# Other begins within a 64 byte line for the operands of three feed-forward stages

## The chip, the cores and the metric

The kernel runs on one core of a Trainium2 chip. The time is that of one execution on the device in microseconds (us), as a median of three runs. The core's engines are TensorE (PE in the profile; its loading of weights has a row of its own, PEld), VectorE (DVE), ScalarE (ACT), GpSimd (POOL) and SyncE (SP), which issues most of the DMAs. All operands lie in the on-chip memory SBUF: 128 partitions, in each of which a tensor occupies a run of bytes. Where such a run begins is what this change is about.

## The reference

A float32 network for 512 positions of width 1024. First four layers, each a mixer (hyena, window attention, pooling, hyena) and a gated feed-forward with an inner width of 2816; then a second block (a gated delta rule beside latent attention, their merge, and a feed-forward with an inner width of 4096). What the change touches are feed-forwards 1 and 2 of the first block and the last feed-forward:

```
def swiglu(xn, wg, wu, wd):
    return (jax.nn.silu(xn @ wg) * (xn @ wu)) @ wd

x = x + swiglu(rmsnorm(x, norm_ffn[i]), ff_w_gate[i], ff_w_up[i], ff_w_down[i])   # layers 0 to 3
...
x = x + mod_x[5] * _sq_relu_mlp(_modulate(_rms(x, norm_mlp[l]), mod_x[3], mod_x[4]), w_mlp_in[l], w_mlp_out[l])
```

## The kernel before, in words

Activations are kept transposed: a row is a tile of 128 features by 512 positions, one feature to a partition, 2048 bytes in each. A matmul takes a weight tile of 128 by 128 (512 bytes in each partition) as its stationary operand and one row as the moved one, 512 columns, and adds into a PSUM bank.

The large products are split. Each operand is written as a high part, rounded to the format fp32r, and a low part, which is what the rounding left, and three fp32r matmuls replace a float32 one (lines 963 to 965): high weights by high rows, high weights by low rows, low weights by high rows. Each of them has its own weight load. So one step over k reads, in this order, `x_hi` with `w_hi`, `x_lo` with `w_hi`, `x_hi` with `w_lo`. The other float32 products of the kernel (lines 1463, 1477 and others) are not split; each of them stands in the trace as two matmuls, the two passes of a float32 product.

A feed-forward (`split_layers`, line 989) runs in parts: two for `ffn`, four for `mlp`. A part has an "in" phase, blocks of weights for two output tiles each, 48 matmuls to a block (11 blocks in `ffn`, 4 in `mlp`), which makes the hidden rows, and an "out" phase of 8 blocks, one output tile each (33 matmuls to a block in `ffn`, 24 in `mlp`), which reads the hidden rows `h_hi` and `h_lo`. A feed-forward has 1584 of these matmuls, the last stage 1536.

Blocks of weights come by DMA from the array `stream` into `ring`, which has four places. ScalarE copies a block rounded into `w_hi` (line 1900), GpSimd writes `w_lo` = ring minus `w_hi` (line 817), and TensorE waits for that. `w_hi` and `w_lo` have two halves, taken in turn by `j % 2`: ScalarE may write half `j % 2` when the matmuls of block j-2 have ended. VectorE writes `x_lo` (lines 2515 and 2520), `h_hi` and `h_lo` (2525 and 2526). All the queues run in the order in which the program was written; each engine's order is fixed by hand.

Tensors lie in SBUF one behind the other in the order of their declaration. `lines` (line 304) rounds the small ones up to 64 elements, 256 bytes, and `before_x` fills 128 bytes so that `x` begins at byte 1280. In the built program every operand of the split products begins at a multiple of 256 bytes. `w_hi`, `x_lo`, `h_hi`, `h_lo`, `w_lo` and `x_hi` lie behind one another in a work area that the other stages use for other things at other times. Feed-forwards 0 and 3 follow a hyena mixer, whose last weights still lie in this area.

Of the kernel before, what the change touches and what calls it, by code (L numbers as in the profile page):

```python
# [24 lines left out]
LINE = 64  # L25
HEAD_GAP = 32
# [265 lines left out]
def build_program(nc, stream, vecs, tabs, tabs2, x_in, ctx_in, first_mods, scratch, x_keep, diag, solved_t, solved_n, out, schedule):  # L292
# [4 lines left out]
    with ExitStack() as stack:  # L297
# [11 lines left out]
        sb("before_x", [P, HEAD_GAP])  # L309
# [444 lines left out]
        def _(pool):  # L754
# [50 lines left out]
            def split(stage, blocks_):  # L805

                def run_(arg):
                    first = starts[(stage, arg)]
                    for j in range(blocks_):
# [7 lines left out]
                        nc.gpsimd.tensor_tensor(w_lo[:, j % 2, 0:cols], ring[:, k % RING, 0:cols], w_hi[:, j % 2, 0:cols],  # L817
# [81 lines left out]
        def _(pe):  # L899
# [82 lines left out]
            def split_weights(j):  # L982

                blk.take()
                n["split"] += 1
                pe.wait_ge(wlo_set, n["split"])
                return [w[:, j % 2, :].rearrange("p (w m) -> p w m", m=P) for w in (w_hi, w_lo)]

            def split_layers(parts, blocks_in, kt_out, mods=False, between=None):

                j = 0
                first = n["xn"] - DT
                for _ in range(parts):
                    for f in range(blocks_in):
                        hi, lo = split_weights(j)
# [8 lines left out]
                    for m in range(DT):  # L1004
                        hi, lo = split_weights(j)
                        split_product(hi, lo, 0, h_hi, h_lo, kt_out, (hidden_set, n["hid"]) if m == 0 else None)
                        j += 1
                    n["hid"] += kt_out

            def ffn(layer):  # L1010
                split_layers(2, FT // 2, FT // 2, True, {2: column_sums, 5: rstd_spread})
# [834 lines left out]
            def mlp(_):  # L1846
                split_layers(4, 4, DT)
# [14 lines left out]
        def _(act):  # L1862
# [30 lines left out]
            def split(stage, arg, j):  # L1893
# [6 lines left out]
                signal(go(w_hi[:, j % 2, 0:cols], ring[:, k % RING, 0:cols], ACT.Copy), whi_set)  # L1900
# [17 lines left out]
            def scaled(k, t, gain):  # L1918
                act.wait_ge(acc_drained[acc.place(t)], acc.turn(t) + 1)
                signal(go(x_hi[:, k, :], x[:, k, :], ACT.Identity, scale=V(gain[0], gain[1] + k)), xhi_set)  # L1920

            def norm(gain, then=None):
# [554 lines left out]
        def _(dve):  # L2477
# [28 lines left out]
            def low(k, high=x_hi, out_=x_lo):  # L2506
# [1066 lines left out]
```

## Time and profile before

| | us |
|---|---|
| median of three runs (lowest, highest) | 4314.81 (4314.14, 4316.48) |
| the profiled execution | 4315.63 |
| its span, first to last instruction | 4313.8 |
| feed-forwards 0 to 3, first to last matmul | 363.8, 363.8, 365.3, 363.8 |
| the last stage, first to last matmul | 356.6 |
| mean granted TensorE clock | 0.957 of full speed |

In a matmul's row the duration is the time from its start to its modelled end. Neighbouring matmuls overlap, so the rate of TensorE is read from the distance of their starts, here called the pitch, and not from the durations. A `x24` in a row of the timeline means that 24 instructions of one form stand in a sequence.

### The profile page before, as it was taken

To read this page: it belongs to the slowest core of one execution; us is meant where nothing else is said; L and a number is where in the kernel's file an instruction comes from. 1 tells how busy PE (TensorE), PEld (TensorE's weight loads), DVE (VectorE), ACT (ScalarE), POOL (GpSimd) and SP (SyncE) were. 2 spreads that over 40 slices of the span, in tenths; PEclk is the share of its full clock that TensorE was granted. 3 is DMA by queue.
4 is the path that set the end of the run, shared out by engine and by line. 5 is a ranking of instruction groups with operands and counts; after the bars stand their busy time and mean duration, and the time that the engine had idled before them with its cause. 6 is when DMAs were issued, how large, how long until landed. Compare 5 with 4: busy or idle time off the path is not lost.

```text
span 4313.8 us, 48957 instructions
## 1 busy us (share of the span) xinstructions
PE 4104.3 (95%) x19446; PEld 3122.4 (72%) x19446; DVE 2207.2 (51%) x3161; ACT 1271.7 (29%) x1756; POOL 1493.9 (35%) x845
## 2 busy tenths in 40 slices
PE   7998999999999999999989998999999999999999
PEld 6655888777888888876568886566666666785887
DVE  6588525475515442576875144566663357404322
ACT  3332222355222322233322222323231234422222
POOL 3311444321444244433124441465663000231443
PEclk9998999999999899999989998999998889999999
DMA  6201332311232223222013321112111111222232
GB/s 185 100 30 40 111 111 83 116 40 69 83 118 85 85 85 124 89 73 88 30 50 126 120 78 68 50 34 58 35 36 55 70 69 69 69 97 72 89 105 76
DMA packets 101075, 341.94 MB, mean 79 GB/s; under 512 B 44400, under 2 KB 47600, under 8 KB 72176
## 3 DMA queue, kind: packets, MB, share of 16 engines
q1 hardware_dynamic: 87968, 311.60, 20.9%
q10 hardware_dynamic: 12880, 27.20, 2.3%
q8 instruction: 155, 2.54, 0.2%
q14 instruction: 72, 0.59, 0.0%
HBM read 321.48 MB, written 17.30 MB: 79 GB/s over the span
## 4 chain that ended last, share of the span: by engine, by line
PE 84%; DVE 10%; ACT 2%; POOL 2%; issue 1%; DMA 0%; SPq 0%; DVEq 0%; ACTq 0%; POOLq 0%
PE bank L963 17%; PE bank L965 17%; PE bank L964 17%; PE bank L1463 5%; PE bank L1175 2%; PE bank L1087 1%; PE bank L1443 1%; PE bank L1165 1%; PE bank L1083 1%; PE bank L927 1%; PE bank L1764 1%; PE bank L1763 1%; PE bank L1785 1%; PE bank L1695 1%; PE bank L1724 1%
## 5 line engine op out<-in xcount | busy, mean ns | idle before, releaser
L817 POOL TENSOR_TENSOR w_lo<-ring,w_hi 128x2048 fp32r<-128x2048 f32 (+2 forms) x200 | 775.6, 3878 | 1187.4 <-ACT w_hi L1900 1158.3
L963 PE MATMUL bank<-x_hi,w_hi 128*128 128x512 f32 x1584 | 617.8, 390 | 3.9 <-POOL w_lo L817 3.9
L965 PE MATMUL bank<-x_hi,w_lo 128*128 128x512 f32 x1584 | 616.7, 389 | 0.0
L964 PE MATMUL bank<-x_lo,w_hi 128*128 128x512 f32 x1584 | 616.6, 389 | 0.0
L1900 ACT ACTIVATE w_hi<-ring 128x2048 fp32r<-128x2048 f32 (+2 forms) x200 | 322.2, 1611 | 713.3 <-PE bank L965 712.3
L963 PE MATMUL bank<-h_hi,w_hi 128*128 128x512 f32 x960 | 374.1, 390 | 0.4
L964 PE MATMUL bank<-h_lo,w_hi 128*128 128x512 f32 x960 | 373.7, 389 | 0.0
L965 PE MATMUL bank<-h_hi,w_lo 128*128 128x512 f32 x960 | 373.7, 389 | 0.0
L963 PEld LDWEIGHTS bank<-x_hi,w_hi 128*128 128x128 f32 x1584 | 297.5, 188 | 66.5 <-POOL w_lo L817 5.2
L964 PEld LDWEIGHTS bank<-x_lo,w_hi 128*128 128x128 f32 x1584 | 297.5, 188 | 61.6
L965 PEld LDWEIGHTS bank<-x_hi,w_lo 128*128 128x128 f32 x1584 | 297.4, 188 | 61.6
L830 POOL TENSOR_TENSOR ring_r<-ring,merge_hi 128x2048 fp32r<-128x2048 f32 x16 | 73.5, 4591 | 494.7 <-ACT merge_hi L2415 494.7
L1463 PE MATMUL bank<-xn,ring 128*128 128x512 f32 x496 | 239.2, 621 | 1.4 <-DVE work L2946 1.4
L2587 DVE TENSOR_TENSOR x<-bank,x 128x512 f32<-128x512 f32 x72 | 49.8, 691 | 355.9 <-PE bank L965 344.5
L963 PEld LDWEIGHTS bank<-h_hi,w_hi 128*128 128x128 f32 x960 | 180.2, 188 | 39.3 <-DVE h_lo L2526 2.0
L964 PEld LDWEIGHTS bank<-h_lo,w_hi 128*128 128x128 f32 x960 | 180.3, 188 | 37.4
L965 PEld LDWEIGHTS bank<-h_hi,w_lo 128*128 128x128 f32 x960 | 180.2, 188 | 37.3
L1978 ACT ACTIVATE xn<-xn 128x512 f32<-128x512 f32 x88 | 55.7, 632 | 453.9 <-DVE xn L2600 453.8
L2600 DVE TENSOR_TENSOR xn<-bank,rstd_t 128x512 f32<-128x512 f32 x88 | 60.8, 691 | 194.1 <-PE bank L965 187.4
L799 POOL TENSOR_TENSOR tab<-tab 56x31 f32<-56x31 f32 (+15 forms) x248 | 151.0, 609 | 19.4
L1463 PEld LDWEIGHTS bank<-xn,ring 128*128 128x128 f32 x496 | 92.7, 200 | 89.8 <-issue 88.6
L854 POOL TENSOR_TENSOR work<-work,ring 128x1024 f32<-128x1024 f32 x32 | 76.7, 2427 | 226.1 <-DVE x L2653 171.1
(527 smaller groups left out, 7889.2 us busy)
## 6 DMA issues: line engine op xcount, KB each, us to landing
ring<-stream SPq DMA_DIRECT2D x211, 1024.0 KB, 4.8
ring<-stream SPq DMA_DIRECT2D x64, 704.0 KB, 4.0
ring<-stream SPq DMA_DIRECT2D x36, 512.0 KB, 3.4
xn<-first_mods SPq DMA_DIRECT2D x8, 1024.0 KB, 6.8
x<-x_keep ACTq DMA_DIRECT2D x3, 2048.0 KB, 8.6
ring<-stream SPq DMA_DIRECT2D x4, 1088.0 KB, 4.9
bias_rows<-work ACTq DMA_DIRECT2D x1, 4096.0 KB, 45.9
x_keep<-x ACTq DMA_DIRECT2D x2, 2048.0 KB, 11.0
```

The source lines that it names most:

```text
L799: solve(tt(part, G[:, 0:i, i:i + 1].broadcast_to([56, i, w]), W[:, i:i + 1, i:SUB].broadcast_to([56, i, w]), ALU.mult))
L817: nc.gpsimd.tensor_tensor(w_lo[:, j % 2, 0:cols], ring[:, k % RING, 0:cols], w_hi[:, j % 2, 0:cols], ALU.subtract).then_inc(wlo_set, 1)
L830: nc.gpsimd.tensor_tensor(ring_r[:, w, 0:2 * DT * P], ring[:, w, 0:2 * DT * P], merge_whi[j % 2][:], ALU.subtract).then_inc(wlo_set, 1)
L854: nc.gpsimd.tensor_tensor(pair, pair, factor[:, r:r + 1, :].broadcast_to([P, 2, 512]), ALU.mult).then_inc(filt_set, 1)
L963: mm(b[:], hi[:, at + k, :], rhs_hi, start=(k == 0), stop=False)
L964: mm(b[:], hi[:, at + k, :], rhs_lo[:, k, :], start=False, stop=False)
L965: ins = mm(b[:], lo[:, at + k, :], rhs_hi, start=False, stop=(k == kt - 1))
L1175: ins = mm(b[:], fwd[term], filt[:, kind, term[1], :], start=(j == 0), stop=(j == 1))
L1463: ins = mm(b[:, 0:TC] if ctx else b[:], w[:, at + k, :], src[:, k, :], start=(k == 0), stop=(k == DT - 1))
L1900: signal(go(w_hi[:, j % 2, 0:cols], ring[:, k % RING, 0:cols], ACT.Copy), whi_set)
L1978: signal(go(gate_tmp[:, f % 2, :], gate_tmp[:, f % 2, :], ACT.Silu), silu_set)
L2600: drain(tt_(gate, bank(t)[:], rstd, ALU.mult), t)
```

## The change

Nothing is added, removed or moved: each engine has the same instructions in the same order, with the same waits. What differs is where tensors begin.

- `LINE` goes from 64 to 16 elements and `before_x` goes away, so the small tensors take less room and everything behind them moves down by 128 to 960 bytes. Each tensor still begins at a multiple of 64 bytes, most of them no longer at one of 256.
- `w_hi` and `w_lo` become two tensors each, one for a half. For feed-forwards 0 and 3 (`EVEN`) the eight pieces lie behind one another as before.
- For feed-forwards 1 and 2 and the last stage the pieces lie in a second layout (names that end in `_at`) over the same area, with 64 bytes of room behind each, and the operands begin some elements into their piece, by the table `BEGIN`. The high rows, `x_hi` and `h_hi`, stay at 0.

The table, written out in elements of 4 bytes past a multiple of 64 bytes:

| stage, phase | low rows | half 0: w_hi, w_lo | half 1: w_hi, w_lo |
|---|---|---|---|
| ffn 1, in | 4 | 0, 0 | 4, 4 |
| ffn 1, out | 8 | 0, 0 | 0, 8 |
| ffn 2, in | 0 | 4, 4 | 8, 8 |
| ffn 2, out | 0 | 2, 2 | 12, 4 |
| last, in | 12 | 0, 0 | 8, 4 |
| last, out | 6 | 0, 0 | 4, 2 |

A row is 2048 bytes and a weight tile 512, so every row and every tile of a tensor begins at the same place of its line.

```diff
-LINE = 64
-HEAD_GAP = 32
+LINE = 16
+PARTS = dict(ffn=FT // 2, mlp=DT)
+PHASE_BLOCKS = dict(ffn=(FT // 2, DT), mlp=(4, DT))
+EVEN = ((0, ((0, 0), (0, 0))), (0, ((0, 0), (0, 0))))
+BEGIN = {
+    ("ffn", 0): EVEN,
+    ("ffn", 1): ((4, ((0, 0), (4, 4))), (8, ((0, 0), (0, 8)))),
+    ("ffn", 2): ((0, ((4, 4), (8, 8))), (0, ((2, 2), (12, 4)))),
+    ("ffn", 3): EVEN,
+    ("mlp", 0): ((12, ((0, 0), (8, 4))), (6, ((0, 0), (4, 2)))),
+}
...
-        sb("before_x", [P, HEAD_GAP])
...
-        w_hi, x_lo, h_hi, h_lo, w_lo, x_hi = [
-            stack.enter_context(nc.sbuf_tensor(name, shape, F32R)) for name, shape in (
-                ("w_hi", [P, 2, 2 * DT * P]), ("x_lo", [P, DT, T]), ("h_hi", [P, FT // 2, T]), ("h_lo", [P, FT // 2, T]),
-                ("w_lo", [P, 2, 2 * DT * P]), ("x_hi", [P, DT, T]))]
+        pieces = (("w_hi0", 2 * DT * P), ("w_hi1", 2 * DT * P), ("x_lo", DT * T), ("h_hi", FT // 2 * T), ("h_lo", FT // 2 * T),
+                  ("w_lo0", 2 * DT * P), ("w_lo1", 2 * DT * P), ("x_hi", DT * T))
+
+        def split_pieces(ending, room):
+            with ExitStack() as over:
+                return {name: over.enter_context(nc.sbuf_tensor(name + ending, [P, size + room], F32R)) for name, size in pieces}
+
+        even_area = split_pieces("", 0)
+        odd_area = split_pieces("_at", LINE)
+        work_end = stack.enter_context(nc.sbuf_tensor("work_end", [P, WORK + len(pieces) * LINE], F32))
+
+        def area(stage, arg):
+            return even_area if BEGIN[stage, arg] is EVEN else odd_area
+
+        def split_rows(name, stage, arg, tiles):
+            at = BEGIN[stage, arg][name[0] == "h"][0] if name.endswith("lo") else 0
+            return area(stage, arg)[name][:, at:at + tiles * T].rearrange("p (a b) -> p a b", a=tiles)
+
+        def split_halves(stage, arg, j):
+            ins, outs = PHASE_BLOCKS[stage]
+            at = BEGIN[stage, arg][j % (ins + outs) >= ins][1][j % 2]
+            return [area(stage, arg)[f"{name}{j % 2}"][:, at[i]:at[i] + 2 * DT * P] for i, name in enumerate(("w_hi", "w_lo"))]
...
-                        nc.gpsimd.tensor_tensor(w_lo[:, j % 2, 0:cols], ring[:, k % RING, 0:cols], w_hi[:, j % 2, 0:cols],
+                        high, low = split_halves(stage, arg, j)
+                        nc.gpsimd.tensor_tensor(low[:, 0:cols], ring[:, k % RING, 0:cols], high[:, 0:cols],
                                                 ALU.subtract).then_inc(wlo_set, 1)
...
-                signal(go(w_hi[:, j % 2, 0:cols], ring[:, k % RING, 0:cols], ACT.Copy), whi_set)
+                signal(go(split_halves(stage, arg, j)[0][:, 0:cols], ring[:, k % RING, 0:cols], ACT.Copy), whi_set)
```

The rest of the diff hands `stage` and `arg` to the functions that read or write these tensors.

## Rows read from the trace of the kernel before

**Rows 1.** The page: span, and engine, busy us (share of the span), instructions.

```profile
span 4313.8 us, 48957 instructions
...
PE 4104.3 (95%) x19446; PEld 3122.4 (72%) x19446; DVE 2207.2 (51%) x3161; ACT 1271.7 (29%) x1756; POOL 1493.9 (35%) x845
```

**Rows 2.** The page's chain that ended last, shares of the span by engine.

```profile
PE 84%; DVE 10%; ACT 2%; POOL 2%; issue 1%; DMA 0%; SPq 0%; DVEq 0%; ACTq 0%; POOLq 0%
```

**Rows 3.** The page's costliest groups: busy, mean ns | idle before, releaser.

```profile
L817 POOL TENSOR_TENSOR w_lo<-ring,w_hi 128x2048 fp32r<-128x2048 f32 (+2 forms) x200 | 775.6, 3878 | 1187.4 <-ACT w_hi L1900 1158.3
L963 PE MATMUL bank<-x_hi,w_hi 128*128 128x512 f32 x1584 | 617.8, 390 | 3.9 <-POOL w_lo L817 3.9
L965 PE MATMUL bank<-x_hi,w_lo 128*128 128x512 f32 x1584 | 616.7, 389 | 0.0
L964 PE MATMUL bank<-x_lo,w_hi 128*128 128x512 f32 x1584 | 616.6, 389 | 0.0
...
L963 PE MATMUL bank<-h_hi,w_hi 128*128 128x512 f32 x960 | 374.1, 390 | 0.4
```

**Rows 4.** Busy time by stretch: feed-forwards 0 to 3, then the last stage.

```profile
core 0: us, PE busy (x) PEld busy (x) DVE busy (x) ACT busy (x) POOL busy (x), PEclk, DMA share, GB/s
443.90:807.70 363.80, 363.80 (x1625) 301.69 (x1623) 151.58 (x172) 85.25 (x72) 155.18 (x38) 1.00 0.30 104
1061.40:1425.20 363.80, 363.80 (x1625) 301.75 (x1623) 148.92 (x173) 83.33 (x71) 151.94 (x37) 1.00 0.30 104
1475.10:1840.40 365.30, 365.30 (x1625) 302.81 (x1625) 148.60 (x172) 83.95 (x71) 155.83 (x38) 1.00 0.30 104
2262.90:2626.70 363.80, 363.80 (x1625) 301.70 (x1623) 147.24 (x172) 83.33 (x71) 152.03 (x37) 1.00 0.29 101
3948.90:4305.50 356.60, 352.27 (x1536) 289.05 (x1536) 119.10 (x141) 84.32 (x84) 140.83 (x46) 0.99 0.24 80
```

**Rows 5.** Line 964, second half of feed-forward 0: durations, first and last start.

```profile
L964 PEld LDWEIGHTS bank<-h_lo,w_hi x88: 187/188/188, 747.8 to 806.9; 128*128 128x128 f32 x88
L964 PE MATMUL bank<-h_lo,w_hi x88: 388/389/390, 748.0 to 807.2; 128*128 128x512 f32 x88
```

**Rows 6.** TensorE in order of time, last stage: start us, us, instruction.

```profile
4100.10 0.39 PE L963 MATMUL bank<-h_hi,w_hi 128*128 128x512 f32 x1
4100.32 0.39 PE L964 MATMUL bank<-h_lo,w_hi 128*128 128x512 f32 x1
4100.55 0.39 PE L965 MATMUL bank<-h_hi,w_lo 128*128 128x512 f32 x1
4100.78 0.39 PE L963 MATMUL bank<-h_hi,w_hi 128*128 128x512 f32 x1
...
4104.18 0.39 PE L963 MATMUL bank<-h_hi,w_hi 128*128 128x512 f32 x1
```

**Rows 7.** Weight loads of the same stretch.

```profile
4100.10 0.19 PEld L964 LDWEIGHTS bank<-h_lo,w_hi 128*128 128x128 f32 x1
4100.33 0.19 PEld L965 LDWEIGHTS bank<-h_hi,w_lo 128*128 128x128 f32 x1
4100.55 0.19 PEld L963 LDWEIGHTS bank<-h_hi,w_hi 128*128 128x128 f32 x1
4100.78 0.19 PEld L964 LDWEIGHTS bank<-h_lo,w_hi 128*128 128x128 f32 x1
```

**Rows 8.** TensorE in order of time, two-pass float32 products, 512 and 256 columns.

```profile
2730.48 10.47 PE L1463 MATMUL bank<-xn,ring 128*128 128x512 f32 x24
2740.78 3.62 PE L1463 MATMUL bank<-work,ring 128*128 128x256 f32 x16
2744.24 2.31 PE L1463 MATMUL bank<-xn,ring 128*128 128x512 f32 x5
```

**Rows 9.** TensorE in order of time, attention: fp32r products of 256 columns.

```profile
897.12 0.28 PE L1217 MATMUL bank<-at_whi,x_hi_a 128*128 128x256 f32 x1
897.23 0.28 PE L1218 MATMUL bank<-ring_r,x_hi_a 128*128 128x256 f32 x1
...
899.27 0.28 PE L1217 MATMUL bank<-at_whi,x_hi_a 128*128 128x256 f32 x1
```

**Rows 10.** TensorE in order of time, recurrent stage: moved tiles at two begins.

```profile
2716.69 0.61 PE L1477 MATMUL bank<-tab,work 128*128 128x128 f32 x4
2717.14 0.39 PE L1473 MATMUL bank<-work 128*128 128x128 f32 x2
2717.36 0.61 PE L1477 MATMUL bank<-tab,work 128*128 128x128 f32 x4
```

**Rows 11.** ScalarE groups by shape.

```profile
L1900 ACT ACTIVATE w_hi<-ring 128x2048 fp32r<-128x2048 f32 x104 | 199.8, 1921 | 283.4 <-PE bank L965 282.7
```

**Rows 12.** GpSimd groups by shape.

```profile
L817 POOL TENSOR_TENSOR w_lo<-ring,w_hi 128x2048 fp32r<-128x2048 f32 x104 | 488.9, 4701 | 746.2 <-ACT w_hi L1900 717.1 <-DVE x_lo L2515 29.1
L817 POOL TENSOR_TENSOR w_lo<-ring,w_hi 128x1408 fp32r<-128x1408 f32 x64 | 210.3, 3285 | 313.1 <-ACT w_hi L1900 313.1
...
L817 POOL TENSOR_TENSOR w_lo<-ring,w_hi 128x1024 fp32r<-128x1024 f32 x32 | 76.5, 2389 | 128.1 <-ACT w_hi L1900 128.1
```

**Rows 13.** Who TensorE waited for in the last stage: us, times, longest.

```profile
PE bank L963 <- POOL w_lo L817: 3.9, 3, 1.3
PE bank L974 <- DVE x_lo L2520: 2.7, 1, 2.7
```

**Rows 14.** Line 817: duration min/median/max, first and last start.

```profile
L817 POOL TENSOR_TENSOR w_lo<-ring,w_hi x200: 2387/4575/5153, 433.0 to 4295.9; 128x2048 fp32r<-128x2048 f32 x52, 128x1408 fp32r<-128x1408 f32 x32, 128x1024 fp32r<-128x1024 f32 x16
```

More of the change, by code:

```diff
@@ L980, in split_pair, with split_weights @@
                         between[k]()
-            def split_weights(j):
+            def split_weights(stage, arg, j):
                 blk.take()
@@ L986, in split_weights, with split_layers @@
                 pe.wait_ge(wlo_set, n["split"])
-                return [w[:, j % 2, :].rearrange("p (w m) -> p w m", m=P) for w in (w_hi, w_lo)]
-            def split_layers(parts, blocks_in, kt_out, mods=False, between=None):
+                return [w.rearrange("p (w m) -> p w m", m=P) for w in split_halves(stage, arg, j)]
+            def split_layers(stage, arg, parts, blocks_in, kt_out, mods=False, between=None):
                 j = 0
+                x_hi, x_lo = [split_rows(name, stage, arg, DT) for name in ("x_hi", "x_lo")]
+                h_hi, h_lo = [split_rows(name, stage, arg, kt_out) for name in ("h_hi", "h_lo")]
                 first = n["xn"] - DT
@@ L994, in split_layers @@
                     for f in range(blocks_in):
-                        hi, lo = split_weights(j)
+                        hi, lo = split_weights(stage, arg, j)
                         if j == 0:
@@ L1010, in ffn @@
             def ffn(layer):
-                split_layers(2, FT // 2, FT // 2, True, {2: column_sums, 5: rstd_spread})
+                split_layers("ffn", layer, 2, FT // 2, FT // 2, True, {2: column_sums, 5: rstd_spread})
             def hyena(s):
@@ L1919, in scaled @@
                 act.wait_ge(acc_drained[acc.place(t)], acc.turn(t) + 1)
-                signal(go(x_hi[:, k, :], x[:, k, :], ACT.Identity, scale=V(gain[0], gain[1] + k)), xhi_set)
+                signal(go(split_rows("x_hi", "ffn", gain[1] // DT, DT)[:, k, :], x[:, k, :], ACT.Identity, scale=V(gain[0], gain[1] + k)), xhi_set)
             def norm(gain, then=None):
@@ L2504, in full, with low @@
                 return t
-            def low(k, high=x_hi, out_=x_lo):
+            def low(k, high, out_):
                 n["xhi"] += 1
@@ L2514, in scaled_low @@
                 dve.wait_ge(xhi_set, n["xhi"])
-                signal(stt(x_lo[:, k, :], x[:, k, :], V(gain[0], gain[1] + k), x_hi[:, k, :], ALU.mult, ALU.subtract), xn_set)
+                high, out_ = [split_rows(name, "ffn", gain[1] // DT, DT) for name in ("x_hi", "x_lo")]
+                signal(stt(out_[:, k, :], x[:, k, :], V(gain[0], gain[1] + k), high[:, k, :], ALU.mult, ALU.subtract), xn_set)
             def shifted_low(k, shift):
@@ L2519, in shifted_low, with split_hidden @@
                 dve.wait_ge(xhi_set, n["xhi"])
-                signal(stt(x_lo[:, k, :], xn[:, k, :], modv[:, shift + k, 0:1], x_hi[:, k, :], ALU.add, ALU.subtract), xn_set)
-            def split_hidden(f):
+                high, out_ = [split_rows(name, "mlp", 0, DT) for name in ("x_hi", "x_lo")]
+                signal(stt(out_[:, k, :], xn[:, k, :], modv[:, shift + k, 0:1], high[:, k, :], ALU.add, ALU.subtract), xn_set)
+            def split_hidden(stage, arg, f):
                 h = h_tmp[:, f % 2, :]
+                h_hi, h_lo = [split_rows(name, stage, arg, PARTS[stage]) for name in ("h_hi", "h_lo")]
                 step(nc.vector.tensor_copy(h_hi[:, f, :], h))
@@ L2605, in ffn @@
                         drain(tt_(h_tmp[:, f % 2, :], bank(t)[:], gate_tmp[:, f % 2, :], ALU.mult), t)
-                        split_hidden(f)
+                        split_hidden("ffn", layer, f)
                         if f in MOD_SUMS:
```

8 lines of the change are left out of this document (4 added, 4 removed).

## The prediction

> **What bounds the kernel now.** I read the page first: TensorE is busy for 95% of the span [rows 1], and the chain that ended last is 84% TensorE [rows 2]. The reader is to see that no other engine can pay for a change here. The costliest groups are the three products of a split step, 1584 + 960 of each, and the idle time ahead of them is 3.9 us and less [rows 3]. By stretches, feed-forwards 0 to 3 take 363.8, 363.8, 365.3 and 363.8 us and the last stage 356.6, all at a granted clock of 0.99 or 1.00, that is at 2.4 GHz, with TensorE busy throughout [rows 4]. The three changed stages are thus 363.8 + 365.3 + 356.6 = 1085.7 us, a quarter of the time, and they hold 1584 + 1584 + 1536 = 4704 split matmuls.
>
> A duration of 390 ns says nothing of the rate, since neighbours overlap. The pitch does: in the last stage 18 pitches lie between 4100.10 and 4104.18 us, 226.7 ns each [rows 6]; in feed-forward 0, 261 pitches lie between the first and last of 88 starts, 59.2 us or 226.8 ns [rows 5]. At 2.4 GHz 512 columns are 213.3 ns. So each split matmul costs 13.3 ns on top of its columns. The fp32r products of 256 columns have 18 pitches in 2.15 us, 119.4 ns, where 256 columns are 106.7: again some 13 ns, so it is an amount per matmul, not a rate [rows 9]. The passes of the unsplit float32 products have pitches of 10.30 us / 24 = 429.2 and 3.46 / 16 = 216.3 ns: their columns go at half the rate (426.7 and 213.3) with about 2.7 ns on top [rows 8]. The weight load of the next matmul starts together with the running one and is over in 190 ns, inside the pitch of 227 [rows 6, 7]. What the change can touch is this overhang: 13.3 - 2.7 = 10.6 ns that only rows streamed at the full rate pay, from columns that are read while weights are read too, all begun at a multiple of 64 bytes.
>
> **The change part by part.** *Instructions:* none is added or moved, so no wait or queue changes; 0 us.
>
> *Low rows begun off the line.* `x_lo` and `h_lo` are displaced for feed-forward 1 (352 in, 176 out) and the last stage (256 and 256): 1040 of the 4704 matmuls move such a row. A row of 2048 bytes touches 33 lines of 64 bytes instead of 32. If the reading goes by such lines, one takes 213.3 / 32 = 6.7 ns at the full rate, and there is nothing to hide it, because the pitch is set by the row: 1040 x 6.7 = +6.9 us. If the line isn't the unit, 0. The trace has no fp32r row off the line. It has float32 tiles of 128 columns off it: line 1473 moves a tile that begins 48 bytes into its line under weights that do so too, line 1477 moves one at 0 under weights at 0, and four of the one take 0.45 us, two of the other 0.22, 112 and 110 ns each [rows 10]. That speaks for 0, but those tiles go at half the rate. I take +1 us, near the row, and keep 0 and 6.9.
>
> *Weights begun off the line.* A load of 512 bytes touches 9 lines instead of 8. It ends 190 ns into a pitch of 227 [rows 7], so up to 37 ns more are hidden: 0. Without that cover each displaced load would cost what it is over.
>
> *Rows and weights at different places of a line.* This is what the table varies. In the order of the reads, a moved row has the load of the next weights beside it: `x_hi` with `w_hi`, `x_lo` with `w_lo`, `x_hi` with `w_hi`. Counting where the two begin at different places: 176 + 352 (ffn 1, in), 88 + 0 (ffn 1, out), 1584 (ffn 2), 128 + 384 and 128 + 384 (last stage), together 3224. If the overhang is a clash of two reads at the same place, they lose up to 10.6 ns each: -34 us. If being at one place is what keeps it small, they gain as much or more: doubled, +34 us. Bounds -34 and +34. The nearest rows, again [rows 10], show no dependence, and the pitch is the same, 226.7, in stages whose rows and weights lie in quite different tensors [rows 5, 6]. I take 0.
>
> The Trainium skill, "SBUF — State Buffer", Who interferes with whom, says that TensorE has two independent read ports, one for the moving operand and one for weights; by that there is no clash and this term is 0. "TensorE: Matmul & The Clock Gate", Back-to-back issue gap, gives N / 2.4 + 2.5 ns, 215.8 for 512 columns; the float32 passes above fit it with their doubled columns, the split matmuls don't, by 10.9 ns. So the pages do not explain the very overhang that this change plays with, and I do not rest on the first rule alone.
>
> *The writers.* ScalarE, GpSimd and VectorE write displaced tensors. A block is rounded in 1.92 us [rows 11] and subtracted in 4.70 [rows 12], 6.6 us, against 48 x 0.2267 = 10.9 us of matmuls for an in block and 33 x 0.2267 = 7.5 for an out block of a feed-forward. Only at the last stage's step from out to in the cover is short, 24 x 0.2267 = 5.4 us, and there TensorE waits today, 3.9 us in 3 times [rows 13]. Were displaced copies slower by the spread of line 817, 5.15 against 4.70 [rows 12, 14], that would be 3 x 0.45 = +1.4 us. I take 0. Faster matmuls would lengthen these waits by 3 x 24 x 0.0106 = 0.8 us.
>
> *All tensors moved down, to multiples of 64 instead of 256 bytes.* The trace has no operand of a split product that isn't at a multiple of 256. If the unit were longer than 64 bytes, feed-forwards 0 and 3 and the mixers would pay as well, with a 33rd of a row, 6.7 ns on each of some 10,000 matmuls, +67 us. Nothing in rows favours that; I take 0 and keep the bound as a rival.
>
> **Sum.** Against the profiled execution: span 4313.8 + 1.8 around it = 4315.6 us; + 1 = 4316.6. The median of the runs is 0.8 lower, 4314.8, so the forecast is 4316 us.
>
> **The rivals.** *Rival 1, the clash is real and is resolved.* For it: the overhang of 10.6 ns exists only where the row is streamed at the full rate, is the same for 256 and 512 columns, as the weight load is, and the rest of the kernel hides it at half rate. Against it: the load runs within each pitch whatever lies where, and its length isn't changed by the begin. With half of the bound, -17 us: 4298; with all of it, 4281. It decides from 8.6 / 3224 = 2.7 ns per matmul.
>
> *Rival 2, slower: rows that begin off the line, or off the place of the weights, break the stream.* A row at the full rate has no slack in which to fetch a second piece; each matmul that it hits gets a longer pitch at once, on the chain. For it: the full-rate stream already pays what the half-rate one doesn't. Against it: [rows 10]. With the overhang doubled on the 1040 displaced low rows, 1040 x 13.3 = +14 us: 4329. On the 3224 with differing places, +34 to +43: 4349 to 4358. At worst the displaced rows fall to the half rate, 1040 x 203 = +211 us. It decides from 8.3 ns on the 1040 or 2.7 ns on the 3224.
>
> *Rival 3, the unit is longer than a line of 64 bytes.* +67 us as worked out, 4382; its mark is that feed-forwards 0 and 3 get longer too.
>
> *By a rule of short lines:* a slower pitch could come only from begins inside a 16 byte line, the 256 out rows of the last stage at element 6, one line of 1.7 ns each, 0.4 us. "SBUF — State Buffer", Specifications, gives SBUF such 16-byte lines. This lies inside the forecast.
>
> **How the numbers follow.** A measurement of this kernel tells apart about 0.2%, 8.6 us. Forecast (0 to +6.9 us, 4313 to 4323): 0.46. Rival 1: 0.26. Rival 2: 0.25. Rival 3: 0.03. Of rival 1 some 0.02 stays within 0.2%, of rival 2 some 0.01. Different begins in twelve places may also pull both ways and cancel, which I count with the forecast. Faster 0.24, same 0.49, slower 0.27. The range leaves out the last fifth of rival 1 (below 4285) and the upper part of rivals 2 and 3 (above 4348): 4285 to 4348. The likeliest case alone: 4313 to 4323.
>
> **What would show it.** Right: feed-forwards 1 and 2 and the last stage again 364, 365 and 357 us, and a pitch of 226.7 ns in all twelve places of the table, with perhaps 233 where a displaced low row is moved. Wrong by rival 1: pitches of 216 to 224 where row and weights differ, and 226.7 where they begin alike (ffn 1, out, half 1), which stays as a control inside the run. Wrong by rival 2: pitches over 230 in the third of the matmuls on line 964 alone, or on all three lines. Feed-forwards 0 and 3 stay at 363.8 in each case but the third. A VectorE, ScalarE or GpSimd group that grew, with TensorE waiting for it, would overturn the term of the writers.

## The result, and the profile after

The changed kernel takes 4350.19 us (median of three, 4347.10 to 4359.28) against 4314.81: a ratio of 1.0086, interval 1.0062 to 1.011. It is slower by 35 us, and the prediction, 4316 with a range of 4285 to 4348, was wrong; the median lies 2 us above the range. The profiled execution took 4347.10 us, its span is 31.5 us longer than that of before.

The page after, in the order of [rows 1] and [rows 3]: span; engines; costliest groups with busy us, mean ns, idle before.

```profile
span 4345.3 us, 48957 instructions
...
PE 4130.2 (95%) x19446; PEld 3111.1 (72%) x19446; DVE 2201.5 (51%) x3161; ACT 1271.4 (29%) x1756; POOL 1496.2 (34%) x845
...
L845 POOL TENSOR_TENSOR w_lo_at<-ring,w_hi_at 128x2048 fp32r<-128x2048 f32 (+2 forms) x124 | 459.7, 3708 | 776.6 <-ACT w_hi_at L1930 768.6
L845 POOL TENSOR_TENSOR w_lo<-ring,w_hi 128x2048 fp32r<-128x2048 f32 (+1 forms) x76 | 317.0, 4171 | 432.0 <-ACT w_hi L1930 412.4
L991 PE MATMUL bank<-x_hi_at,w_hi_at 128*128 128x512 f32 x912 | 361.6, 396 | 3.5 <-POOL w_lo_at L845 3.5
L992 PE MATMUL bank<-x_lo_at,w_hi_at 128*128 128x512 f32 x912 | 359.8, 394 | 0.0
L993 PE MATMUL bank<-x_hi_at,w_lo_at 128*128 128x512 f32 x912 | 358.2, 393 | 0.0
L991 PE MATMUL bank<-x_hi,w_hi 128*128 128x512 f32 x672 | 261.8, 390 | 0.0
```

The instructions are the same in number, TensorE has 26 us more of busy time and no other engine has grown by more than GpSimd's 2.3 us: GpSimd's two groups make 776.7 us together, against 775.6 in [rows 3], and TensorE waits for them 3.5 us instead of 3.9. The matmuls themselves take longer: in the moved stages 393 to 396 ns each, in the two that were left alone 390 as before.

Feed-forwards 0 to 3 and the last stage after, to be held against [rows 4]:

```profile
core 0: us, PE busy (x) PEld busy (x) DVE busy (x) ACT busy (x) POOL busy (x), PEclk, DMA share, GB/s
445.50:809.30 363.80, 363.75 (x1625) 301.63 (x1623) 152.43 (x172) 85.16 (x72) 157.47 (x38) 1.00 0.29 104
1063.50:1436.40 372.90, 372.90 (x1625) 302.17 (x1623) 148.56 (x172) 83.27 (x71) 152.32 (x37) 1.00 0.29 101
1480.20:1856.50 376.30, 376.28 (x1624) 303.19 (x1624) 148.57 (x174) 83.96 (x71) 151.72 (x38) 0.99 0.28 100
2280.80:2644.60 363.80, 363.77 (x1625) 301.63 (x1623) 148.05 (x172) 83.25 (x71) 154.17 (x37) 1.00 0.29 101
3972.60:4336.80 364.20, 360.65 (x1536) 289.44 (x1536) 118.55 (x141) 84.31 (x84) 141.35 (x46) 0.99 0.23 78
```

The granted clock is that of before, 0.99 to 1.00. Feed-forwards 0 and 3 have not changed. The three moved stages are longer, and from the start of the first matmul to that of the last (the ends are modelled) the traces give +9.0, +11.0 and +7.5 us, together 27.5. (Feed-forward 2 takes 365.7 to 366.1 us in e1 and e7 to e9 below, where nothing in it is displaced, against 364.9 before, so about 1 us of its 11.0 is no matter of the layout.) That is 27.5 / 4704 = 5.8 ns per split matmul.

Matmuls in order of time (start us, us), and one row of line 991 by count, first and last start. First feed-forward 0, then the last six pitches of feed-forward 1, then the last stage; against [rows 5] and [rows 6]:

```profile
L991 PE MATMUL bank<-h_hi,w_hi x88: 389/389/389, 749.2 to 808.4; 128*128 128x512 f32 x88
...
1434.61 0.40 PE L993 MATMUL bank<-h_hi_at,w_lo_at 128*128 128x512 f32 x1
1434.84 0.40 PE L991 MATMUL bank<-h_hi_at,w_hi_at 128*128 128x512 f32 x1
1435.08 0.40 PE L992 MATMUL bank<-h_lo_at,w_hi_at 128*128 128x512 f32 x1
1435.31 0.40 PE L993 MATMUL bank<-h_hi_at,w_lo_at 128*128 128x512 f32 x1
...
1436.02 0.39 PE L993 MATMUL bank<-h_hi_at,w_lo_at 128*128 128x512 f32 x1
...
4100.11 0.40 PE L991 MATMUL bank<-x_hi_at,w_hi_at 128*128 128x512 f32 x1
...
4102.21 0.40 PE L991 MATMUL bank<-x_hi_at,w_hi_at 128*128 128x512 f32 x1
```

Feed-forward 0: 59.2 us / 261 = 226.8 ns, as before. At the end of feed-forward 1, in the blocks that the prediction named as its control, 1.41 us / 6 = 235 ns. In the last stage 2.10 / 9 = 233 ns. In most steps all three products are longer, also that of `x_hi` with `w_hi` where both tensors begin at element 0 of their piece. Not everywhere: in the half 0 blocks of feed-forward 1's out phase the third product, `h_hi` with `w_lo`, keeps 226.8 ns (mean of 88), while the step as a whole takes 693 ns instead of 680.

The rest of the 31.5 us lies outside the feed-forwards. From the same two traces, in us:

| stretch | before | after | difference |
|---|---|---|---|
| start to feed-forward 0 | 443.9 | 445.5 | +1.6 |
| feed-forwards 0 and 3 | 727.0 | 726.7 | -0.3 |
| mixer ahead of ffn 1 | 254.0 | 254.7 | +0.7 |
| feed-forward 1 | 363.5 | 372.5 | +9.0 |
| pooling ahead of ffn 2 | 50.3 | 44.2 | -6.1 |
| feed-forward 2 | 364.9 | 375.9 | +11.0 |
| mixer ahead of ffn 3 | 422.8 | 424.7 | +1.9 |
| second block to its last stage | 1322.6 | 1328.4 | +5.8 |
| last stage | 356.2 | 363.8 | +7.5 |
| behind the last matmul | 8.6 | 8.9 | +0.3 |

The -6.1 is the clock, not the change. The end of the pooling stage, before and then after:

```profile
1457.00:1475.10 18.10, 18.10 (x90) 18.10 (x89) 13.36 (x14) 10.23 (x12) 4.55 (x1) 0.51 0.00 1
```

```profile
1468.00:1480.10 12.10, 9.68 (x87) 9.59 (x86) 11.68 (x13) 9.98 (x12) 4.63 (x1) 0.92 0.10 28
```

Some 90 matmuls in each. Before they ran at a granted 0.51 (the lower level, 1.2 GHz), after mostly at 2.4. In other runs this stretch fell to either side whatever the layout, 44.2 to 53.5 us in all, so I count it as neither gain nor loss. Without it the mixers and the second block cost about +10 us. By these lengths alone that is not certain: among runs in which the split products outside the feed-forwards keep the pitch of before, the second block takes 1321.3 us (e9) to 1327.2 us (e10). The mixers and the second block also hold split products, 2784 of them, whose operands lie in `xn`, `ring` and the work area. A mixer of before and the same of after (lines 974 to 976 have become 1002 to 1004):

```profile
31.00 0.39 PE L974 MATMUL bank<-x_hi_h,early_hi 128*128 128x512 f32 x1
...
32.81 0.39 PE L976 MATMUL bank<-x_hi_h,ring_r 128*128 128x512 f32 x1
```

```profile
31.03 0.40 PE L1002 MATMUL bank<-x_hi_h,early_hi 128*128 128x512 f32 x1
...
32.88 0.39 PE L1004 MATMUL bank<-x_hi_h,ring_r 128*128 128x512 f32 x1
```

Eight pitches each: 226 ns and 231 ns. 2784 x 4.4 = 12 us is what this would cost throughout. Taken pitch by pitch over the two traces (2630 pairs of neighbouring starts, less than 0.3 us apart), the split products outside the feed-forwards take 231.4 instead of 227.3 ns, which is 10.9 us. That is the loss outside the feed-forwards.

**The layout as it was built.** The pitch did not follow the table of begins, so I worked out every operand's byte address modulo 256. Before: 0 for all. After:

| | place modulo 256 bytes |
|---|---|
| `x`, `xn`, `ring` | 128 |
| work area, and the pieces of ffn 0 and 3 | 64 |
| `w_hi0`, `w_hi1`, `x_lo`, `h_hi` of the moved stages | 64, 128, 192, 0 (+ table) |
| `h_lo`, `w_lo0`, `w_lo1`, `x_hi` of the moved stages | 64, 128, 192, 0 (+ table) |

The room of 64 bytes behind each piece moves the next one by a whole line, so rows and weights lie at different places of 256 bytes even where the table says 0 and 0. And the smaller header moved `xn` and `ring` by another amount than the work area. Both stand in the diff; the prediction read past both.

The unsplit float32 products of after, as [rows 8]:

```profile
2748.83 10.46 PE L1493 MATMUL bank<-xn,ring 128*128 128x512 f32 x24
2759.13 3.62 PE L1493 MATMUL bank<-work,ring 128*128 128x256 f32 x16
2762.58 5.74 PE L1493 MATMUL bank<-xn,ring 128*128 128x512 f32 x13
```

10.30 / 24 = 429 and 3.45 / 16 = 216 ns, as before. The first is no test, since `xn` and `ring` both lie at 128; the second is one, for `work` (64) and `ring` (128) now lie at different places. Lines 1195 (`ring` 128, `work` 64) and 1205 (`work` 64, `tab` 192) are one for 512 columns: their starts are 429 ns apart, as before. What slows the split products leaves the half-rate ones alone.

Nor does it slow the fp32r products of 256 columns in the attention stage, to be held against [rows 9]. `x_hi_a` now lies at 64, `ring_r` and `xn_r` at 128 and `at_whi` at 64, so two of the three products have their row and weights at different places:

```profile
899.32 0.28 PE L1247 MATMUL bank<-at_whi,x_hi_a 128*128 128x256 f32 x1
...
901.45 0.28 PE L1247 MATMUL bank<-at_whi,x_hi_a 128*128 128x256 f32 x1
```

18 pitches in 2.13 us are 118.3 ns, against 119.4 before. So the loss is shown for fp32r products of 512 columns only.

### The profile page after: what moved, and what is told of

The parts are those of the page before. It is cut to its first block, busy times and chain, and to the rows that moved or that the text cites. A ratio compares the mean times of both kernels' runs of the same rounds, so it can differ in the third digit from the quotient of the medians.

```text
span 4345.3 us, 48957 instructions
## 1 busy us (share of the span) xinstructions
PE 4130.2 (95%) x19446; PEld 3111.1 (72%) x19446; DVE 2201.5 (51%) x3161; ACT 1271.4 (29%) x1756; POOL 1496.2 (34%) x845
## 4 chain that ended last, share of the span: by engine, by line
PE 84%; DVE 10%; ACT 2%; POOL 2%; issue 1%; DMA 0%; SPq 0%; DVEq 0%; ACTq 0%; POOLq 0%
PE bank L991 18%; PE bank L992 17%; PE bank L993 17%; PE bank L1493 5%; PE bank L1205 2%; PE bank L1117 1%; PE bank L1473 1%; PE bank L1195 1%; PE bank L1113 1%; PE bank L955 1%; PE bank L1794 1%; PE bank L1793 1%; PE bank L1815 1%; PE bank L1725 1%; PE bank L1754 1%
## 5 line engine op out<-in xcount | busy, mean ns | idle before, releaser
L845 POOL TENSOR_TENSOR w_lo_at<-ring,w_hi_at 128x2048 fp32r<-128x2048 f32 (+2 forms) x124 | 459.7, 3708 | 776.6 <-ACT w_hi_at L1930 768.6
L845 POOL TENSOR_TENSOR w_lo<-ring,w_hi 128x2048 fp32r<-128x2048 f32 (+1 forms) x76 | 317.0, 4171 | 432.0 <-ACT w_hi L1930 412.4
L991 PE MATMUL bank<-x_hi_at,w_hi_at 128*128 128x512 f32 x912 | 361.6, 396 | 3.5 <-POOL w_lo_at L845 3.5
L992 PE MATMUL bank<-x_lo_at,w_hi_at 128*128 128x512 f32 x912 | 359.8, 394 | 0.0
L993 PE MATMUL bank<-x_hi_at,w_lo_at 128*128 128x512 f32 x912 | 358.2, 393 | 0.0
L991 PE MATMUL bank<-x_hi,w_hi 128*128 128x512 f32 x672 | 261.8, 390 | 0.0
L992 PE MATMUL bank<-x_lo,w_hi 128*128 128x512 f32 x672 | 261.4, 389 | 0.0
L993 PE MATMUL bank<-x_hi,w_lo 128*128 128x512 f32 x672 | 261.4, 389 | 0.0
L991 PE MATMUL bank<-h_hi_at,w_hi_at 128*128 128x512 f32 x608 | 241.9, 398 | 0.0
L992 PE MATMUL bank<-h_lo_at,w_hi_at 128*128 128x512 f32 x608 | 239.9, 395 | 0.0
```

The lines of the kernel that those rows point to most:

```text
L845: nc.gpsimd.tensor_tensor(low[:, 0:cols], ring[:, k % RING, 0:cols], high[:, 0:cols], ALU.subtract).then_inc(wlo_set, 1)
L991: mm(b[:], hi[:, at + k, :], rhs_hi, start=(k == 0), stop=False)
L992: mm(b[:], hi[:, at + k, :], rhs_lo[:, k, :], start=False, stop=False)
L993: ins = mm(b[:], lo[:, at + k, :], rhs_hi, start=False, stop=(k == kt - 1))
```

## The experiments

Below, "place" is an address modulo 256 bytes, and a stage's length is from its first to its last matmul's start. "Sum of three" is the time from one high by high product to the next, three matmuls: 680 ns in every stage of before, as the median.

**e1: the changed kernel with every stage even.** No room, no table; the small header stays.

```diff
-BEGIN = {
-    ("ffn", 0): EVEN,
-    ("ffn", 1): ((4, ((0, 0), (4, 4))), (8, ((0, 0), (0, 8)))),
...
+BEGIN = {key: EVEN for key in (("ffn", 0), ("ffn", 1), ("ffn", 2), ("ffn", 3), ("mlp", 0))}
```

> The changed kernel with its smaller small tensors (LINE 16, no 128 byte gap), but every stage in the even layout: no room behind the pieces, no begin inside a line. All tensors begin at multiples of 64 bytes; those of the work area are at 320 modulo 512, x, xn and ring at 128. Theory A (pitch is 226.7 ns only where all rows and weights of a step begin at the same place of something longer than 64 bytes): feed-forwards 1, 2 and the last stage go back to 363.5, 365 and 356 us, the mixers and the merge stay at 231.1 ns on 2784 matmuls, 12 us over before: about 4325 us. Theory B (only begins inside a 64 byte line cost): 4315, with 226.7 everywhere; that the mixers' triples of 693 ns in the changed kernel were something else would then have to be shown.

Measured 4325.45 against 4317.02 us, ratio 1.0024 (1.0014 to 1.0033). Feed-forward 1 and the last stage:

```profile
1065.80:1429.60 363.80, 363.74 (x1625) 301.63 (x1623) 149.34 (x172) 83.24 (x71) 154.11 (x37) 1.00 0.30 104
3957.70:4314.80 357.10, 352.47 (x1536) 289.07 (x1536) 119.87 (x141) 84.30 (x84) 142.94 (x46) 0.99 0.24 80
```

The feed-forwards are back, and about a quarter of the loss stays. It lies in the other stages, where the sum of three is 693 ns; counted pitch by pitch as above, their split products take 11.0 us longer than before.

**e2: the changed kernel with 320 bytes of filler ahead of the work area**, so that it lies at the place of `xn` and `ring` (and at the same one modulo 512).

```diff
+        sb("filler", [P, 80])
         with nc.sbuf_tensor("at_whi", [P, 2, 2 * DT * P], F32R) as at_whi:
```

> The changed kernel with 320 bytes of filler ahead of the work area, so that the work area, x, xn and ring all lie at 128 modulo 512; table and rooms of the three changed stages as in the changed kernel. Theory A: mixers and merge return to 226.7 ns, the three stages keep their +9, +11 and +7.5 us: about 4350 - 12 = 4338 to 4342 us. Theory B: no change against the changed kernel, 4350.

Measured 4339.28, ratio 1.0054 (1.0039 to 1.0069). The mixers' sum of three is 680 again, with not one instruction changed in them, only moved by 320 bytes, and their split products take as long as before (0.0 us, counted pitch by pitch). The span is 8.0 us shorter than after's, 4337.3. The three stages keep their loss: 371.8, 375.9, 363.5 us.

**e3: e2 with all begins 0, and only the rooms left.**

```diff
+ZERO = ((0, ((0, 0), (0, 0))), (0, ((0, 0), (0, 0))), "at")
-    ("ffn", 1): ((4, ((0, 0), (4, 4))), (8, ((0, 0), (0, 8)))),
+    ("ffn", 1): ZERO,
...
```

> As the run with the filler, but every begin of the table is 0: no operand begins inside a line. What is left of the change in the three stages is the 64 bytes of room behind each piece, which puts the eight pieces at eight different multiples of 64 modulo 512. Theory A: the stages stay at 231 to 233 ns, within some us of the run with the filler: 4335 to 4342 us. Theory B: 226.7 ns in all stages, 4315 us.

Measured 4344.53, ratio 1.0067 (1.0052 to 1.0082). Feed-forwards 1 and 2, last stage:

```profile
1061.50:1434.90 373.40, 373.40 (x1625) 302.02 (x1623) 148.90 (x173) 83.35 (x71) 152.18 (x37) 1.00 0.29 101
1480.00:1855.80 375.80, 375.76 (x1624) 303.75 (x1624) 149.83 (x174) 83.97 (x71) 156.27 (x38) 0.99 0.29 100
3969.50:4333.90 364.40, 360.81 (x1536) 289.34 (x1536) 118.23 (x141) 84.37 (x84) 141.24 (x46) 0.99 0.24 78
```

The median is 2.5 us above what theory A expected. Every operand begins at a multiple of 64 bytes, no row touches a 33rd line, and the loss of the three stages is whole: 27.8 us against 27.5. So whole lines of distance are enough.

**e5: the table alone.** Pieces put in another order and padded so that all lie at one place modulo 256; what differs are the 8 to 48 bytes of the table.

```diff
+            ("ffn", 1): split_pieces("_at1", ("w_hi0", "x_lo", "w_hi1", "h_lo", "h_hi", "w_lo0", "x_hi", "w_lo1"), dict(w_hi1=64, h_hi=64)),
+            ("ffn", 2): split_pieces("_at2", ("w_hi0", "w_hi1", "x_lo", "h_hi", "h_lo", "x_hi", "w_lo0", "w_lo1"), dict(x_lo=64)),
...
```

> The changed kernel's table, in layouts in which all pieces of the three stages lie at the same place modulo 256 bytes (and so do x, xn and ring), so that operands differ by their begin inside a 64 byte line alone. Theory T1, from the map (either difference is enough, by whole lines below 256 bytes or inside a line, and they do not add up): the three stages stay at 230 to 233 ns, except where one weight part alone is off by 4 elements: about 4335 to 4345 us. Theory T2 (whole lines alone cost, begins inside a line do nothing by themselves): 4315 to 4318 us, the three stages 363.5, 365 and 356 us.

Measured 4336.44 against 4315.59, ratio 1.0046 (1.0029 to 1.0063).

```profile
1060.90:1431.90 371.00, 371.00 (x1625) 302.22 (x1623) 148.95 (x173) 83.29 (x71) 152.31 (x37) 1.00 0.29 102
1477.10:1852.70 375.60, 375.60 (x1624) 305.08 (x1624) 148.57 (x174) 84.00 (x71) 151.80 (x38) 0.99 0.28 100
3964.30:4329.00 364.70, 361.05 (x1536) 289.45 (x1536) 117.97 (x141) 84.35 (x84) 141.16 (x46) 1.00 0.23 78
```

Differences inside the line cost as much as whole lines do (+7.2, +10.3, +8.1 us), and the two do not add up: e2 has both, and its three stages sum to 1111.3 us, between the 1110.3 of e5 and the 1112.4 of e3. By itself e5 does not tell a distance inside the line from a place that is no multiple of 32 bytes, which costs too (e10). Where only multiples of 32 occur, the distance still costs: with `h_lo` alone 32 bytes off (feed-forward 1, out, half 0) the sum of three is 696, and the cells 0, 8, 8 and 8, 0, 0 of the map below have 699 and 700.

**e4 and e6: maps.** With the header of before, the "out" phases of the four feed-forwards and all phases of the last stage take one layout each: some 30 cells a run, 27 to 44 steps each. The "in" phases of the feed-forwards stay as before, 680.

```diff
+PLAN = {
+    ("ffn", 0): dict(x=(0, 0), h=((0, 0), (0, 0)), w=((((0, 0), (0, 0)), ((0, 0), (128, 128))), (((0, 0), (0, 0)), ((16, 16), (32, 32))))),
...
+            at = PLAN[stage, arg]["w"][part][at >= ins][j % 2]
```

> The layout of before (all tensors at the same place modulo 512), and 32 different begins in one run: in the out phases of feed-forwards 0 to 3 only weights are shifted (by 2 to 128 elements), in the last stage rows too. Sum of three pitches is 680 ns where nothing differs. Theory A: 680 where both weights move by 128 elements (512 bytes), and where rows and weights move together by 16 or by 4 elements; 693 to 700 where they differ by 16, 32, 64 or 96 elements; and begins inside a line, 2 to 12 elements, cost as much as whole lines or nothing, but not more. Theory B: over 680 only for 2, 4, 8 and 12 elements, also where rows and weights move together; 680 for 16, 32, 64 and 96. A third, that the moved row alone counts, gives 680 in all feed-forwards. Time 4320 to 4340 us.

> A second map in the layout of before: 32 begins in one run. T1: three pitches sum to 680 ns with the low rows 64 elements (256 bytes) off and all else at 0, also with w_hi 64 off; 690 to 700 for odd begins (1 element), for 6, 20, 24, 40, 56 and 60 elements, and for rows and weights together at 8 or at 2 elements; 680 again for one weight part alone at 4. If any begin gives less than 680, there is a layout better than that of before; T1 has 680 as the floor. If 60 elements (4 below the next multiple) cost less than 4, the order of rows and weights matters and not their distance. Whole run 4330 to 4345 us.

One execution each, 4333.97 and 4329.34 us, which says nothing of a cell. The cells, as the median sum of three in ns. Begins are in elements of 4 bytes, in the order low row, `w_hi`, `w_lo`, past the high row at 0:

| begins | sum | begins | sum |
|---|---|---|---|
| 0, 0, 0 | 680 | 0, 128, 128 (512 bytes) | 680 |
| 0, 64, 64 (256 bytes) | 680 | 64, 0, 0 / 64, 64, 0 | 680 / 680 |
| 0, 16, 16 | 700 | 0, 32, 32 | 695 |
| 0, 96, 96 | 699 | 0, 0, 16 / 0, 16, 0 | 693 / 700 |
| 0, 0, 32 | 694 | 0, 8, 8 / 0, 12, 12 | 699 / 700 |
| 0, 4, 4 / 0, 2, 2 / 0, 1, 1 | 700 / 693 / 696 | 0, 60, 60 | 684 |
| 0, 0, 4 / 0, 4, 0 | 680 / 680 | 0, 0, 1 / 0, 0, 8 | 700 / 700 |
| 4, 0, 0 | 693 | 16, 0, 0 / 8, 0, 0 | 700 / 700 |
| all four at 16 | 680 | all four at 8 | 680 |
| all four at 4 | 700 | all four at 2 | 694 |

From e4, feed-forward 3 with `w_hi` 16 bytes off (0, 4, 0):

```profile
2587.20 0.39 PE L998 MATMUL bank<-h_hi,w_hi 128*128 128x512 f32 x1
...
2594.68 0.39 PE L998 MATMUL bank<-h_hi,w_hi 128*128 128x512 f32 x1
```

33 pitches in 7.48 us, 226.7 ns. And feed-forward 2 with `w_hi` 64 bytes off (0, 16, 0):

```profile
1606.41 0.40 PE L998 MATMUL bank<-h_hi,w_hi 128*128 128x512 f32 x1
...
1611.32 0.40 PE L998 MATMUL bank<-h_hi,w_hi 128*128 128x512 f32 x1
```

21 pitches in 4.91 us, 234 ns, and the third product pays too, whose row and weights (`h_hi`, `w_lo`) lie at one place; what is loaded beside it, the next `w_hi`, is 64 bytes off. From the map I read four things. No cell is below 680: the layout of before is at the floor of what was tried. 680 comes back at distances of 256 and 512 bytes. A lone weight tile 16 bytes off costs nothing, while one 4, 32 or 64 bytes off does; I have no reason for that. And the direction of the distance matters, which answers a question that the second map was to settle: 60 elements (4 short of the next 256 bytes) cost less than 4, 684 against 700, and 48 less than 16, 687 against 700. With 684, and with 703 for 24 elements, two cells lie outside the 690 to 700 expected.

**e7: e1 with 64 bytes of filler.** It puts the work area at the place of `xn` and `ring` modulo 256, but not modulo 512, and nothing at a multiple of 256.

```diff
+        sb("filler", [P, 16])
         with nc.sbuf_tensor("at_whi", [P, 2, 2 * DT * P], F32R) as at_whi:
```

> The run with the even layout and the small header, plus 64 bytes ahead of the work area: work area at 384 modulo 512, x, xn and ring at 128, so alike modulo 256 but not modulo 512, and nothing at a multiple of 256. If what counts is the distance modulo 256 bytes: 226.7 ns in mixers and merge too, 4315 to 4318 us, the time of before. If it is modulo 512, or a begin at a multiple of 256: about 4325 us.

Measured 4321.07 against 4315.87 us, ratio 1.0006 (0.9996 to 1.0015): the median is above the 4315 to 4318 expected, the interval holds the time of before. Its profiled span, 4308.9 us, is 14.4 shorter than that of e1, but it is that of the shortest of ten executions, so the 14.4 is not the price of the 64 bytes. Counted pitch by pitch, the split products outside the feed-forwards take 11.0 us more than before in e1 and 0.1 in e7; the rest lies in gaps between phases. A mixer of e7, and the same of e1:

```profile
100.11 0.39 PE L986 MATMUL bank<-x_hi_h,z_lo 128*128 128x512 f32 x1
...
102.83 0.39 PE L986 MATMUL bank<-x_hi_h,z_lo 128*128 128x512 f32 x1
```

```profile
100.16 0.39 PE L985 MATMUL bank<-x_hi_h,z_lo 128*128 128x512 f32 x1
...
102.95 0.39 PE L985 MATMUL bank<-x_hi_h,z_lo 128*128 128x512 f32 x1
```

12 pitches each: 226.7 and 232.5 ns. What counts here is the distance modulo 256, not 512, and no begin has to be a multiple of 256.

**e8 and e9: the kernel before with `HEAD_GAP` 36 and 40**, meant to move everything together by 16 and by 32 bytes.

```diff
-HEAD_GAP = 32
+HEAD_GAP = 36
```

> The kernel before, unchanged but for the gap ahead of x: 36 elements instead of 32, so that every tensor behind it begins 16 bytes further on, all together; no distance between two of them changes. If distances alone count: 4315 us. If the begin of a moved row inside a piece of 32 bytes counts by itself, as the map's place with everything at 4 elements says (697 instead of 680 ns for three): 5.7 to 6.7 ns on each of 10656 matmuls, 60 to 70 us, about 4380 us.

> As the run with 36 elements, with 40: everything 32 bytes further on together. The map's place with everything at 8 elements gave 680 ns. If the unit of the begin is 32 bytes: 4315 us, as before. If it is the line of 64 bytes, so that a row touches one line more: again about 4380 us.

Measured 4315.63 and 4316.92 against 4315.87, ratios 1.0 (0.999 to 1.0009) and 1.0002 (0.9993 to 1.0011). But tensors are placed at multiples of 32 bytes: the built program of e8 has them where e9 has them. So the two are one layout. It shows that all together 32 bytes further costs nothing, and the expectation for 16 bytes was not tried by it. e10 does that.

**e10: all operands 16 bytes further, together.** The header and the order of pieces are those of before; only the high and low rows and weights of the three stages begin 4 elements into their piece.

```diff
+MOVED = "moved"
+ROWS, WEIGHTS = 4, 4
+BEGIN = {("ffn", 0): EVEN, ("ffn", 1): MOVED, ("ffn", 2): MOVED, ("ffn", 3): EVEN, ("mlp", 0): MOVED}
```

> The kernel before with its own header and its own order of pieces; only, in feed-forwards 1 and 2 and the last stage, every operand of the split products (high and low rows, high and low weights) begins 16 bytes further. All distances between operands stay as before. A: only distances modulo 256 bytes count: all five stages as before (363.5, 363.5, 364.9, 363.5, 356.2 us), 4316 us. B: a common begin that is not at a multiple of 32 bytes costs too, as the places with all four operands at 4 elements showed (233 ns instead of 226.7): 4704 x 6.7 ns = +31 us in the three moved stages, 4347 us, with feed-forwards 0 and 3 as before.

Measured 4337.74 against 4313.99 us, ratio 1.005 (1.0034 to 1.0067).

```profile
1058.70:1431.10 372.40, 372.40 (x1625) 301.93 (x1623) 148.92 (x173) 83.31 (x71) 152.25 (x37) 1.00 0.29 101
1476.20:1851.40 375.20, 375.16 (x1624) 304.05 (x1624) 149.82 (x174) 83.95 (x71) 156.37 (x38) 0.99 0.28 100
3966.70:4328.70 362.00, 358.15 (x1536) 288.79 (x1536) 118.63 (x141) 84.31 (x84) 141.53 (x46) 0.99 0.24 79
```

B holds: +8.5, +9.9, +5.4 us with no distance changed at all. The price is 5.1 ns per matmul (23.8 / 4704), somewhat below the 6.7 expected. So the common place counts as well: 16 bytes cost here and 8 in the map, while 0, 32 (e8), 64 (map, and feed-forwards 0 and 3 of after) and 128 (e7) cost nothing. All of the free ones are multiples of 32; 24 bytes was not tried.

**e11: weights 64 bytes from the rows.** Everything begins at a multiple of 64 bytes.

```diff
+MOVED = "moved"
+ROWS, WEIGHTS = 0, 16
+        moved_area = split_pieces("_at", ROOM, ('x_hi', 'x_lo', 'h_hi', 'h_lo', 'w_hi0', 'w_hi1', 'w_lo0', 'w_lo1'), 0)
```

> The kernel before with its own header; in feed-forwards 1 and 2 and the last stage the pieces lie in another order and the four weight pieces, high and low, begin 64 bytes (one whole line) past a multiple of 256, the rows at multiples of 256. Everything begins at a multiple of 64 bytes. A, the distance from rows to weights modulo 256 bytes counts: pitch 233 ns in all three stages, 4704 x 6.7 = +31 us, 4347 us. B, only begins inside a 64 byte line count (the wrong reading that the table suggests): all stages as before, 4316 us. Feed-forwards 0 and 3 stay at 363.5 us in both.

Measured 4346.93 us, ratio 1.0072 (1.0057 to 1.0087). The three stages, and nine pitches of the last one:

```profile
1061.40:1435.60 374.20, 374.20 (x1625) 301.24 (x1623) 148.74 (x173) 83.40 (x71) 151.83 (x37) 1.00 0.29 101
1485.50:1861.00 375.50, 375.50 (x1625) 302.26 (x1625) 148.44 (x172) 84.02 (x71) 155.98 (x38) 1.00 0.29 101
...
3972.70:4338.20 365.50, 362.00 (x1536) 289.06 (x1536) 118.10 (x141) 84.33 (x84) 140.94 (x46) 0.99 0.23 78
```

```profile
4100.03 0.40 PE L997 MATMUL bank<-x_hi_at,w_hi_at 128*128 128x512 f32 x1
...
4102.13 0.39 PE L997 MATMUL bank<-x_hi_at,w_hi_at 128*128 128x512 f32 x1
```

A holds: 2.10 / 9 = 233 ns in the last stage, +10.3, +10.2 and +8.8 us, 29.4 in all. One whole line of distance, with nothing off a line anywhere, makes this kernel about as slow as the change did. That the pieces also lie in another order does not matter for this: the map's cell 0, 16, 16 has the same distance in the order of before, and the same 700 ns for three. Another 3.4 us of the span lie in the mixer ahead of feed-forward 3. They are not the split products, whose pitches outside the feed-forwards sum to those of before (0.0 us), and e10 with the same mixers has 2.2 us there.

## Why the prediction was wrong

*What bounds the kernel: right.* TensorE, with the pitch of the split matmuls, sets the time; the loss is all in TensorE's rows.

*Rows and weights at different places, taken as 0: this step failed.* It is worth +27.5 us in the three stages. I valued it from [rows 10], float32 tiles of 128 columns at half rate, which showed no dependence, and from the equal pitch of stages whose operands lie "in quite different tensors" [rows 5, 6]. The first rows were of the wrong kind: a split matmul takes 233 ns in e11, while the half-rate products of after keep their 216 and 429. In the built program the tiles of line 1477 in [rows 10] do lie at different places modulo 256, the row at 0 and the weights at 128 and 64, and at half rate this shows nothing. The second were no test, because all those tensors lay at the same place modulo 256. I had the fact that every operand begins at a multiple of 256 bytes and did not see that, in consequence, the trace held no case of what I was valuing.

*The count of places, 3224 matmuls: wrong.* I counted differences in the table and left out the rooms behind the pieces. All 4704 have their row and their weights at different places, and every kind of step pays, 688 to 707 ns for three, though not each of its matmuls. The control that I named (ffn 1, out, half 1) was none: `h_hi` lies at 0 and `w_hi1` at 128, and it ran at 235 ns.

*Rival 2 was the case.* Its mechanism (begins off the place of the weights lengthen each pitch at once) is what came. That its size, +34 us on 3224 matmuls, is near the 35 measured is luck: 5.8 ns instead of 10.6, on 4704 instead of 3224, make 27.5 us, and the rest came from the mixers, which it did not name. It put "off the line" first; e3 and e11 show that nothing needs to be off a line.

*Low rows off the line, +1: no term of its own.* A low row 16 bytes off costs 13 ns per three matmuls in the map, but so do weights with the row on its line, and e5 and e3 do not add up.

*Weights off the line, 0 because the load is hidden: wrong with its reason.* The load still takes 188 ns (`x_lo_at` with `w_hi_at`, as in [rows 5]) and ends inside the pitch, and the pitch grows all the same: 700 ns for three with `w_lo` alone 32 bytes off.

*All tensors moved down, 0: wrong by about 11 us.* The bound of +67 and rival 3 assumed a longer unit, at which every operand off a multiple of 256 pays, with feed-forwards 0 and 3 as the mark. These stayed at 363.35 us, all at place 64, so rival 3 as it was priced is refuted; its premise, that more than the 64 byte line counts, is what e3 and e11 show, for distances. The cost came elsewhere: `xn` and `ring` moved by another amount than the work area, and the mixers' split products pay 231 ns. e2 and e7 take that away with a filler.

*The writers, 0: right.* VectorE, ScalarE and GpSimd take what they took, and the waits did not grow.

The Trainium skill, "SBUF — State Buffer", Who interferes with whom, gives TensorE two independent read ports, for the moved operand and for the weights. By that the distance between the two should not matter, and the term was 0; e11 measures 6.3 ns per matmul for a distance of 64 bytes. The measurement decides. It does not show that the two reads collide. If a row clashed with its own weights, the third product of the cell 0, 16, 0 would not pay, and it takes 235 ns. If it clashed with the weights loaded beside it, the second product of the cell 0, 0, 16 would pay most and the third nothing; they take 229 and 236 ns. And e10 pays with all distances kept.

**Open.** Which part of the read makes the pitch 230 to 236 ns instead of 226.7 is not settled. The rule (one place modulo 256, that place a multiple of 32) holds for the fp32r products of 512 columns in e1 to e3, e5, e7 to e11 and the cells, apart from a lone weight tile 16 bytes off, which is free. Why those of 256 columns don't pay is open. Why the floor is 226.7 and not 216, as half-rate products of 256 columns have, is open too; no begin among some 60 cells lowered it. A version faster than the kernel before was not found.

## What to carry to other kernels

A stream of fp32r matmuls of 512 columns that is bound by its pitch wants its rows and its weights to begin at the same place modulo 256 bytes in the partition, and that place at a multiple of 32; here nearly anything else cost 1 to 9 ns, mostly 4 to 7, on the average matmul of 227. After any change in the tensors' list, work out all operand addresses from the built program: padding, a removed filler or room behind a tensor shifts everything behind it. And before a term is set to 0 "because the rows show no dependence", check that the rows hold a case in which the thing varies, for instructions of the same rate.

## What was not expected of the hardware

- 64 bytes of filler, in no feed-forward's way, were worth 11 us of the mixers' and the second block's split products (e1 to e7); the ratios went from 1.0024 to 1.0006.
- One displaced operand can lengthen all three products of a step, unequally (236, 229, 235 ns for 0, 16, 0).
- The two commonest pitches, 226.7 and 233.3 ns, differ by 6.7, a 32nd of a row's 213.3, though no row touches another line in e11.
- Half-rate float32 products, 216 and 429 ns, did not react to different places, nor did fp32r products of 256 columns, 118 ns.
- At the end of the pooling stage the granted clock is 0.51 in some executions and 0.92 in others, which moves the span by up to 9 us whatever the layout.
